# A hybrid SSD, pooling and expert layer on one core: expert outputs added into the residual by accumulating DMAs, weights of ranked experts loaded after the first gathers

## The chip, the cores and the metric

The kernel runs on one core of a Trainium2 chip. The metric is the device time of one execution in microseconds (us). The engines are TensorE (PE; its weight loads are shown as PEld), VectorE (DVE), ScalarE (ACT), GpSimd (POOL) and SyncE (SP). DMAs are issued by SP, ACT and POOL, each on a queue of its own, and run on 16 DMA engines. An indirect DMA takes a table of row numbers from on-chip memory, and POOL issues it.

## What is computed

One layer over 640 tokens of 1024 features (128 context, 512 latent), all float32. A first half (modulated norm, projections, two-way SSD scan, pooling mixer, output projection) leaves a residual `x`. The second half, which the change is about, routes each token to two of 16 experts and adds their weighted sum, gated, to the residual; a last norm gives the output:

```python
combine = jnp.sum(one_hot(idx, N_EXPERTS) * gate[..., None], axis=1)   # two gates a token
g = jnp.einsum("td,edf->tef", t, w_gate)
u = jnp.einsum("td,edf->tef", t, w_up)
a = silu(g) * u * combine[..., None]
out = jnp.einsum("tef,efd->td", a, w_down)
x = x + gate2 * out          # gate2: one row for context tokens, one for latent tokens
y = rmsnorm(x, final_norm_w)
```

## The kernel before

**Slots and tiles.** After routing, DVE ranks the experts by their number of tokens and gives every (token, choice) pair a slot. A tile holds up to 128 slots of one expert; a unit is 32 slots. The experts run in a fixed order of ranks (`RUN_ORDER`), 51 units in all: 47 written out (`UNITS`, 16 tiles in `TILES`), and a tile of 4 units in a loop that repeats if experts have more tokens than their space (here it runs once). `token_of` holds, for each tile, the token number of each slot.

**One tile.** POOL gathers the tile's token rows from `h2_dram` with an indirect DMA (`gather`, L1376) into one of two buffers `xg`; it issues the gather of tile q as soon as tile q-2 has been turned (`s_xtp`, L1383). PE turns the rows feature-major (`turn_tokens`, L872) during the last unit of the tile before; ACT and DVE copy the result out of PSUM (L1175, L1837).

**One unit.** PE multiplies by gate and up weights (`gate_up`, L882: two stretches with the turn of the unit before between them), ACT applies silu (L1182), DVE multiplies (`activate`, L1841), PE turns the activation (L887), ACT copies it (L1179), PE multiplies by the down weights (`down`, L895) into one of two PSUM banks, and DVE copies the 128x256 result (32 slots by 4 column groups of 256 on 128 partitions) into a buffer `yo` of its tile (`copy_out`, L1844). PE's `down` of unit v waits until the output of unit v-2 has been copied (`s_yo`). DVE works strictly in this order: `activate(v)`, then `unit_out(v-1)`.

**Storing.** When a tile's last unit is copied, ACT stores the tile with four DMAs, one per column group, to `slot_out` in DRAM (`store`, L1187; the loop's tile L1236). There are two `yo` buffers: the first copy into one waits until the tile two before has been stored:

```python
def unit_out(v):
    n, q, u = UNITS[v]
    dve.wait_ge(s_dn, v + 1)
    if u == 0 and q >= 2:
        dve.wait_ge(s_yst[q % 2], 64 * (q // 2))      # L1850
    copy_out(v, q % 2, u)
```

**Weights.** Each expert has six chunks of 1 MB (`w_exp`); 16 chunk slots stand on chip. Expert 0's are loaded ahead. As soon as the order of experts is known (`s_own`, L488), SP loads the next ones (L495), ten chunks at once and then each when its slot has been used for the last time.

**The end.** When all tiles are stored, POOL gathers for each of the five token tiles the two rows of each token from `slot_out` (10 indirect DMAs, L1401). ACT weights the first rows (`weigh`, L1243), DVE mixes (`mix`, L1892), POOL multiplies by gate2 (L1409), DVE adds to the residual `x1` on chip (`residual`, L1901), ACT sums squares and takes the root (L1251, L997), DVE normalises into one of two buffers `fout` (`final_norm`, L1909), and SP stores `y_out` (L504).

**Earlier places that the change touches.** POOL clears the rows of `slot_out` that no slot fills with 24 DMAs (L1344, at 170 to 182 us). After each output-projection tile ACT stores h2 (`copy_h2`, L1148). At the end of routing DVE builds one-hot tables (L1811 to L1813), PE sums them into token numbers (L861, 20 matmuls), and DVE casts these to `token_of` (L1829), which releases POOL's first gathers.

Of the kernel before, what the change touches and what calls it, by code (L numbers as in the profile page):

```python
# [23 lines left out]
F32 = mybir.dt.float32  # L24
# [41 lines left out]
SLOTS = MAX_TILES * P  # L66
# [20 lines left out]
UNFILLED = [(t * P + size * TU, (t + 1) * P) for t, size in TILES if size < 4]  # L87
UNFILLED += [(t * P, (t + 1) * P) for t in range(MAIN_TILES, MAX_TILES)]
# [13 lines left out]
C_STACK, C_KEY, C_TAB = 722, 754, 770  # L102
C_ALL = 818
# [24 lines left out]
def trunk_kernel(nc, consts, bconsts, vecs, rows, inv, fnorm, x, states0, w_ring, w_late, b_late, w_dt,  # L128
                 w_pool, w_router, w_exp, y_out, s_out):
    ctx = ExitStack()  # L130
    with ctx:
# [9 lines left out]
        slot_out = nc.dram_tensor("slot_out", [SLOTS, D], F32).ap()  # L141
# [213 lines left out]
        s_yst = [sem(f"expert_outputs_stored_{i}") for i in range(2)]  # L355
        s_yg = [sem(f"expert_rows_gathered_{j}") for j in range(NJ)]
        s_ya = sem("first_rows_weighted")
        s_mix = sem("expert_rows_mixed")
        s_gm = sem("mixed_rows_gated")
        s_fin = sem("final_sum_ready")  # L360
# [25 lines left out]
        yo = [t.rearrange("p (u c) -> p u c", u=4) for t in (zf[:, 4 * D:5 * D], bf_[:, 0:D])]  # L386
# [3 lines left out]
        g2row = rf[:, 0:2 * D].rearrange("p (c d) -> p c d", c=2)  # L390
        fnrow = rf[:, 2 * D:3 * D]
        fout = [rf[:, 3 * D + i * D:3 * D + (i + 1) * D] for i in range(2)]
        ygb = ex[:, 0:2 * NJ * D].rearrange("p (n d) -> p n d", d=D)
        ri = sb("ri", [P, 64], I32)
        idx = sb("idx", [P, 2], I32)
# [7 lines left out]
        in_tile = zf[:, 3328:3328 + 2 * NJ * MAX_TILES].rearrange("p (i n) -> p i n", n=MAX_TILES)  # L403
# [7 lines left out]
        def _(sp):  # L411
# [76 lines left out]
            sp.wait_ge(s_own, 1)  # L488
            for n in range(1, E - 1):
# [7 lines left out]
            with sp.Fori(0, k_loop) as i:  # L497
                e = sp.value_load(ri[0:1, bass.ds(i + E, 1)], min_val=0, max_val=E - 1)
                sp.wait_ge(s_lrel, i + 1)
                for c in range(6):  # L500
                    sp.dma_start(slots_[LOOP_SLOT + c], w_exp[e, c]).then_inc(s_ch[LOOP_SLOT + c], 16)
            for j in range(NJ):
                sp.wait_ge(s_fo, j + 1)
                sp.dma_start(y_out[j * P:(j + 1) * P, :], fout[j % 2]).then_inc(s_ost[j % 2], 16)  # L504
# [6 lines left out]
        def _(pe):  # L511
# [348 lines left out]
            for i in range(2 * NJ):  # L860
                mm = pe.matmul(psb[5][:, 0:MAX_TILES], at_pos[:, i, :], in_tile[:, i, :],  # L861
# [57 lines left out]

            pe.wait_ge(s_xg[0], 16)  # L920
# [72 lines left out]
        def _(act):  # L993
# [148 lines left out]
            def copy_h2(j):  # L1142
# [5 lines left out]
                act.dma_start(h2_dram[j * P:(j + 1) * P, :], h2bufs[j % 2]).then_inc(s_h2s[j % 2], 16)  # L1148

# [16 lines left out]
            copy_h2(NJ - 1)  # L1166
            exp_logits(1)
            warm(ACT.Silu)

# [13 lines left out]

            def store(rows, b, size):

                for g in range(AG):
                    act.dma_start(slot_out[rows, g * 256:(g + 1) * 256].rearrange("(u t) c -> t u c", t=TU),  # L1187
                                  yo[b][g * TU:(g + 1) * TU, 0:size, :]).then_inc(s_yst[b], 16)
# [3 lines left out]
            for v, (n, q, u) in enumerate(UNITS):  # L1192
# [12 lines left out]
                if v >= 2 and UNITS[v - 2][2] == TILES[UNITS[v - 2][1]][1] - 1:  # L1205
                    qs = UNITS[v - 2][1]
                    t, size = TILES[qs]
                    act.wait_ge(s_yo, v - 1)
                    store(slice(t * P, t * P + size * TU), qs % 2, size)
# [3 lines left out]
            act.wait_ge(s_yo, NV)  # L1213
            t, size = TILES[NQT - 1]
            store(slice(t * P, t * P + size * TU), (NQT - 1) % 2, size)
            act.dma_start(fnrow, fnorm.to_broadcast([P, D])).then_inc(s_fn, 16)
# [28 lines left out]
            for j in range(NJ - 1):  # L1245
                weigh(j)
# [775 lines left out]
```

## Time and profile before

| what | value |
|---|---|
| time, median of 3 runs | 986.18 us (985.52 to 986.61) |
| profiled execution, its own time | 986.62 us |
| its span, first to last instruction | 984.4 us |
| busy: PE, DVE, ACT, POOL | 858.6, 368.0, 166.6, 221.8 us |
| DMA traffic over the span | 199.61 MB, mean 203 GB/s |
| experts, first PE turn of tokens to last copy out | 626.85 to 937.06 us |
| after the experts, to the end of the span | 47.3 us |

The stretch before 600 us is the first half and the routing begins at its end; the experts take some 310 us; the tail gathers, mixes, norms and stores. A row of the timeline gives start, length, engine, line, what it writes and reads, and in brackets the idle time of the engine before it with what ended that.

### The profile page before, as it was taken

What the parts mean: (1) busy time and instruction counts of PE and PEld (TensorE: products, weight loads), DVE (VectorE), ACT (ScalarE), POOL (GpSimd) and SP (SyncE); (2) the same over time, 40 slices, a digit from 0 to 9 for tenths busy, and PEclk for the clock granted to TensorE, in tenths of its full rate; (3) what the DMA queues carried; (4) which work ended last, traced back from release to release, by engine and by line L of the source; (5) the groups of instructions that cost most, each with busy time, mean ns of one, the idle gap of its engine ahead of it and who ended that gap; (6) DMA issues with size and microseconds to landing.
All of it is one profiled execution on the core that took longest, in us unless ns stands there. A gap on an engine that the chain in (4) does not pass through costs nothing.

```text
span 984.4 us, 18375 instructions
## 1 busy us (share of the span) xinstructions
PE 858.6 (87%) x7969; PEld 491.2 (50%) x7969; DVE 368.0 (37%) x651; ACT 166.6 (17%) x367; POOL 221.8 (23%) x255
## 2 busy tenths in 40 slices
PE   1899999999899999999999972499998999999900
PEld 1655555555545555554445542255555555555500
DVE  1431004543683799873223527011111111111128
ACT  4121001121312222220000210011111111111123
POOL 0169999400233333320000000100000000000062
PEclk9999999999999999999999985699999999999965
DMA  9932755950310000295000011989989999998262
GB/s 357 414 137 95 311 194 188 351 216 7 123 42 0 1 1 1 94 371 200 21 22 21 21 62 46 380 334 357 362 308 418 336 390 399 388 406 311 82 234 107
DMA packets 39551, 199.61 MB, mean 203 GB/s; under 512 B 4720, under 2 KB 13872, under 8 KB 22320
## 3 DMA queue, kind: packets, MB, share of 16 engines
q1 hardware_dynamic: 22032, 162.82, 42.1%
q0 software_dynamic: 6224, 22.55, 6.5%
q10 hardware_dynamic: 11216, 13.08, 4.0%
q8 instruction: 63, 1.03, 0.4%
q14 instruction: 16, 0.13, 0.0%
HBM read 176.37 MB, written 22.05 MB: 202 GB/s over the span
## 4 chain that ended last, share of the span: by engine, by line
PE 55%; DVE 11%; DMA 3%; issue 2%; POOL 1%; ACT 1%; ACTq 0%; POOLq 0%; DVEq 0%
PE bank L882 18%; PE bank L782 13%; PE bank L895 8%; PE bank L646 6%; DMA slot_out<-yT 2%; PE bank L872 2%; PE bank L887 1%; DVE ex L1559 1%; PE bank L684 1%; DVE xs L1612 1%; DVE ex L1892 1%; DMA yT<-h_dram,token_of 1%; PE bank L835 1%; POOL ex L1367 1%; DVE ex L1575 1%
## 5 line engine op out<-in xcount | busy, mean ns | idle before, releaser
L574 PE MATMUL bank<-hT,ring 128*128 128x512 f32 (+1 forms) x640 | 180.7, 442 | 1.5 <-DMA ring<-w_ring 1.5
L574 PEld LDWEIGHTS bank<-hT,ring 128*128 128x128 f32 x640 | 96.6, 194 | 73.5 <-issue 71.0
L1376 POOL DMA_INDIRECT yT<-h_dram,token_of x17 | 16.6, 979 | 423.6 <-PE bank L872 236.4
L1841 DVE TENSOR_TENSOR bcT<-bcT,bank 128x128 f32<-128x128 f32 x51 | 14.6, 287 | 176.3 <-ACT bcT L1182 176.3
L646 PE MATMUL bank<-ring,hT 128*128 128x512 f32 x160 | 75.2, 604 | 4.5 <-DVE ex L1583 2.2
L882 PE MATMUL bank<-ex,yT 128*32 128x256 f32 x1216 | 74.7, 388 | 0.8 <-DVE yT L1837 0.8
L882 PE MATMUL bank<-ring,yT 128*32 128x256 f32 x1248 | 75.1, 381 | 0.0
L782 PE MATMUL bank<-ring,yT 128*128 128x512 f32 x160 | 70.2, 593 | 0.8 <-DVE yT L1621 0.8
L1367 POOL TENSOR_TENSOR ex<-ex,dts 128x512 f32<-128x512 f32 x40 | 44.3, 1108 | 99.9 <-ACT ex L1116 99.7
L882 PEld LDWEIGHTS bank<-ex,yT 128*32 128x32 f32 x1216 | 37.5, 112 | 27.3 <-issue 2.4
L882 PEld LDWEIGHTS bank<-ring,yT 128*32 128x32 f32 x1248 | 37.9, 110 | 25.4 <-issue 0.3
L782 PEld LDWEIGHTS bank<-ring,yT 128*128 128x128 f32 x160 | 30.3, 190 | 38.8 <-issue 37.8
L646 PEld LDWEIGHTS bank<-ring,hT 128*128 128x128 f32 x160 | 28.2, 190 | 31.6 <-issue 25.9
L1575 DVE TENSOR_TENSOR ex<-ex,gT 128x512 f32<-128x512 f32 x40 | 31.9, 797 | 24.3 <-POOL ex L1367 24.3
L895 PE MATMUL bank<-ex,bcT 128*32 128x256 f32 x640 | 38.2, 379 | 0.0
L1116 ACT ACTIVATE ex<-bank 128x512 f32<-128x512 f32 x40 | 23.9, 597 | 83.5 <-PE bank L733 83.4
L1179 ACT ACTIVATE bcT<-bank 128x128 f32<-128x128 f32 x51 | 14.2, 277 | 139.0 <-PE bank L887 139.0
L1746 DVE COPY bcT<-bank 128x512 f32<-128x512 f32 x10 | 6.9, 692 | 78.2 <-PE bank L782 78.2
L782 PE MATMUL bank<-ring,uT 128*128 128x512 f32 x80 | 36.1, 597 | 0.0
L782 PE MATMUL bank<-hT,uT 128*128 128x512 f32 x80 | 35.3, 594 | 0.8 <-DVE bcT L1600 0.8
L1351 POOL TENSOR_TENSOR ex<-xs,dts 128x1024 f32<-128x1024 f32 x8 | 15.1, 1901 | 87.4 <-DVE xs L1500 70.0
L1512 DVE SCALAR_TENSOR_TENSOR ex<-ex,vec 128x643 f32<-128x643 f32 x36 | 33.0, 916 | 1.3
(286 smaller groups left out, 1185.2 us busy)
## 6 DMA issues: line engine op xcount, KB each, us to landing
ex<-w_exp SPq DMA_DIRECT2D x36, 1024.0 KB, 11.8
ring<-w_exp SPq DMA_DIRECT2D x36, 1024.0 KB, 12.6
ring<-w_ring SPq DMA_DIRECT2D x13, 2048.0 KB, 10.5
yT<-w_late SPq DMA_DIRECT2D x16, 1024.0 KB, 6.5
hT<-w_exp SPq DMA_DIRECT2D x12, 1024.0 KB, 13.7
uT<-w_exp SPq DMA_DIRECT2D x12, 1024.0 KB, 15.6
slot_out<-ex POOLq DMA_DIRECT2D x13, 512.0 KB, 16.6
ex<-x SPq DMA_DIRECT2D x5, 512.0 KB, 8.0
```

Of the source, the lines that this page charges most:

```text
L574: mm = pe.matmul(o, w[:, k, (f % 4) * P:(f % 4 + 1) * P], hT[:, k, lo:hi], start=(k == 0), stop=(k == KT - 1))
L646: mm = pe.matmul(psb[6][:, :], hT[:, k, j * P:(j + 1) * P], w[:, k, :], start=(k == 0), stop=(k == KT - 1), skip_group_check=True)
L782: mm = pe.matmul(out_bank(j, hf_, c)[:, :], (yT, uT)[c][:, k, j * P:(j + 1) * P], w[:, k, :], start=(k == 0), stop=(k == KT - 1), skip_gro ...
L872: mm = pe.transpose(psb[2 + k // 4][:, (k % 4) * P:(k % 4) * P + rows], xg[b][0:rows, k * P:(k + 1) * P], ident[0:rows, 0:rows])
L882: mm = pe.matmul(psb[v % 2][g * TU:(g + 1) * TU, 0:256], xgT[b][:, k, u * TU:(u + 1) * TU], w[:, kk, g, :], start=(k == 0), stop=(k == KT ...
L895: mm = pe.matmul(psb[6 + v % 2][g * TU:(g + 1) * TU, 0:256], aT[v % 2][:, fb * TU:(fb + 1) * TU], w[:, kk, g * 256:(g + 1) * 256], start=( ...
L1116: act.activation(wbuf(i)[:, :, :, :], psb[4 + i % 2][:, :].rearrange("p (h d t) -> p h d t", h=2, d=2), ACT.Exp).then_inc(s_ex, 1)
L1351: return pool.tensor_tensor(out.rearrange("p (h d) -> p h d", d=HD), x_.rearrange("p (h d) -> p h d", d=HD), factors.unsqueeze(2).to_broad ...
L1367: pool.tensor_tensor(wbuf(i)[:, :, :, :], wbuf(i)[:, :, :, :], dt_h.unsqueeze(3).to_broadcast([P, 2, 2, P]), ALU.mult).then_inc(s_wd, 1)
L1376: pool.indirect_dma_start(xg[b][0:size * TU, :], None, h2_dram, bass.IndirectOffsetOnAxis(ap=numbers, axis=0), bounds_check=TOK - 1, oob_i ...
L1512: ins = stt(cacc[f % 2], xpad[f % 2][:, q:q + 643], wq, cacc[f % 2], ALU.mult, ALU.add)
L1575: step(tt(w.rearrange("p h d t -> p (h d) t"), w.rearrange("p h d t -> p (h d) t"), gT[:, j, hh // HG, :].unsqueeze(1).to_broadcast([P, 4, ...
```

## The change

**Adding in DRAM.** The residual `x1` is also stored to a DRAM tensor `x2_dram` (by ACT in `copy_h2`, five DMAs of 512 KB; the tensor has 128 spare rows for slots that hold no token). Seen as rows of 256 columns, 4 to a token, it takes each unit's 128x256 output by one indirect DMA from POOL that adds (`add_rows`). Before an output leaves PSUM, DVE multiplies it by gate and gate2: `weigh` makes a 128x256 row of weights by two instructions, and `copy_out` is now a multiplication (three DVE instructions of 128x256 instead of one). Outputs go to `YB = 4` buffers of one unit each.

**What waits for what.** POOL issues the add of unit v when its output stands (`s_yo`) and the add of unit v-1 has landed (`s_sc`). DVE's copy of unit v waits until the add of unit v-4 has landed. The gather of tile q+2 now stands in POOL's program behind the add of the unit before tile q's first. The stores to `slot_out`, its gathers, `weigh`, `mix`, `residual` and the 24 clearing DMAs are gone (one clearing DMA is left). At the end SP waits for the last add, loads the five tiles from `x2_dram`, and norm and store follow.

**Routing.** The table that PE sums gets twice the columns (token code and gate: 60 instead of 30), DVE does two more instructions before it and two more behind it, ahead of the first gather. Beside the first gathers, PE spreads the values over partitions (16 matmuls) and DVE makes weights and row numbers of all units.

**Weights.** SP loads the ranked experts' chunks only when both first gathers have landed (`s_xg`).

```diff
@@ SP
             sp.wait_ge(s_own, 1)
+            sp.wait_ge(s_xg[0], 16)
+            sp.wait_ge(s_xg[1], 16)
             for n in range(1, E - 1):
...
+            sp.wait_ge(s_sc, k_loop * 64 + 16 * NV)
+            for j in range(NJ):
+                sp.dma_start(x1[:, j, :], x2_dram[j * P:(j + 1) * P, :]).then_inc(s_x2[j], 16)
@@ ACT
                 act.dma_start(h2_dram[j * P:(j + 1) * P, :], h2bufs[j % 2]).then_inc(s_h2s[j % 2], 16)
+                act.dma_start(x2_dram[j * P:(j + 1) * P, :], x1[:, j, :]).then_inc(s_acc, 16)
...
-                    act.wait_ge(s_yo, v - 1)
-                    store(slice(t * P, t * P + size * TU), qs % 2, size)
...
-            for j in range(NJ - 1):
-                weigh(j)
             for j in range(NJ):
-                act.wait_ge(s_fin, j + 1)
+                act.wait_ge(s_x2[j], 16)
                 act.activation(junk_z, x1[:, j, :], ACT.Square, accum_out=stat[:, j:j + 1]).then_inc(s_fss, 1)
@@ POOL
-            for lo, hi in UNFILLED:
-                pool.dma_start(slot_out[lo:hi, :], zero_f[0:hi - lo, :]).then_inc(s_zero, 16)
+            pool.dma_start(x2_dram[TOK:TOK + P, :], zero_f).then_inc(s_zero, 16)
...
-            for q, (t, size) in enumerate(TILES):
-                if q >= 2:
-                    pool.wait_ge(s_xtp, q - 1)
+            x2_parts = x2_dram.rearrange("r (g n) -> (r g) n", g=AG)
+            def add_rows(numbers, b):
+                pool.indirect_dma_start(x2_parts, bass.IndirectOffsetOnAxis(ap=numbers, axis=0), yo[b], None,
+                                        bounds_check=(TOK + P) * AG - 1, oob_is_err=True,
+                                        compute_op=ALU.add).then_inc(s_sc, 16)
+            def gather_tile(q):
+                t, size = TILES[q]
                 gather(token_of[0:size * TU, t:t + 1], q % 2, size)
+            gather_tile(0)
+            gather_tile(1)
+            pool.wait_ge(s_acc, 16 * NJ)
+            pool.wait_ge(s_zero, 16)
+            pool.wait_ge(s_slot, 1)
+            for v, (n, q, u) in enumerate(UNITS):
+                if u == 0 and q + 2 <= NQT:
+                    pool.wait_ge(s_xtp, q + 1)
+                    gather_tile(q + 2)
+                pool.wait_ge(s_yo, v + 1)
+                if v >= 1:
+                    pool.wait_ge(s_sc, 16 * v)
+                c = TILES[q][0] * 4 + u
+                add_rows(rows_of[:, c:c + 1], v % YB)
             with pool.Fori(0, k_loop) as i:
                 pool.wait_ge(s_xg[LB], i * 16 + 16 * (NQT // 2 + 1))
+                pool.wait_ge(s_sc, i * 64 + 16 * NV)
...
@@ DVE
+            def weigh(done, ctx_col, lat_col):
+                ts(weight_q, g2q[:, 0, :], ctx_col, None, ALU.mult).then_inc(s_wq, 1)
+                dve.wait_ge(s_wq, done + 1)
+                stt(weight_q, g2q[:, 1, :], lat_col, weight_q, ALU.mult, ALU.add).then_inc(s_wq, 1)
+                dve.wait_ge(s_wq, done + 2)
-            def copy_out(v, b, u):
-                dve.tensor_copy(yo[b][:, u, :], psb[6 + v % 2][:, 0:256]).then_inc(s_yo, 1)
+            def copy_out(v):
+                tt(yo[v % YB], psb[6 + v % 2][:, 0:256], weight_q, ALU.mult).then_inc(s_yo, 1)
             def unit_out(v):
...
+                weigh(2 * v, w_ctx[:, c:c + 1], w_lat[:, c:c + 1])
                 dve.wait_ge(s_dn, v + 1)
-                if u == 0 and q >= 2:
-                    dve.wait_ge(s_yst[q % 2], 64 * (q // 2))
+                if v >= YB:
+                    dve.wait_ge(s_sc, 16 * (v - YB + 1))
```

In the loop tile the same waits stand with the loop's count added; there DVE, after the first `activate`, also waits until POOL has copied that tile's weights, which POOL does only when all 47 adds before have landed.

**How the order moves.** POOL's program before, from the first gather on (h_dram is h2_dram, token_of the table of row numbers, yT holds the buffers `xg`):

```order
L1376 DMA yT<-h_dram,token_of 128x1024
L1376 DMA yT<-h_dram,token_of 96x1024
L1376 DMA yT<-h_dram,token_of 128x1024
L1376 DMA yT<-h_dram,token_of 64x1024
L1376 DMA yT<-h_dram,token_of 128x1024
L1376 DMA yT<-h_dram,token_of 32x1024
```

The same stretch of POOL's program now (x_dram is x2_dram, its rows are 256 wide; yT,bcT hold the outputs and the row numbers):

```order
L1367 DMA yT<-h_dram,token_of 128x1024
L1367 DMA yT<-h_dram,token_of 96x1024
L1367 DMA yT<-h_dram,token_of 128x1024
L1376 DMA x_dram<-yT,bcT 3072x256 x4
L1367 DMA yT<-h_dram,token_of 64x1024
L1376 DMA x_dram<-yT,bcT 3072x256 x3
L1367 DMA yT<-h_dram,token_of 128x1024
L1376 DMA x_dram<-yT,bcT 3072x256 x4
```

Where POOL's queue held only gathers, one add per unit now stands between them, and each gather from the third on stands behind the adds of the tile before.

DVE's program at the beginning of the experts before (the first tile's tokens, then two activations ahead of the first copy out; bcT holds the activations, yT tokens and outputs):

```order
L1837 COPY yT<-bank 128x512
L1841 TENSOR_TENSOR bcT<-bcT,bank 128x128 x2
L1844 COPY yT<-bank 128x256
L1841 TENSOR_TENSOR bcT<-bcT,bank 128x128
L1844 COPY yT<-bank 128x256
L1837 COPY yT<-bank 128x4x96
```

And now:

```order
L1851 COPY yT<-bank 128x512
L1855 TENSOR_TENSOR bcT<-bcT,bank 128x128 x2
L1859 TENSOR_SCALAR bcT<-bcT 128x256
L1861 SCALAR_TENSOR_TENSOR bcT<-bcT 128x256
L1865 TENSOR_TENSOR yT<-bank,bcT 128x256
L1855 TENSOR_TENSOR bcT<-bcT,bank 128x128
```

Two instructions of 128x256 have come between the activation and the copy out, which has become a multiplication; the rest of a unit stands where it stood.

## Rows read from the trace of the kernel before

**Rows 1.** Windows: busy us (instructions) of each engine, granted clock, DMA share, GB/s.
```profile
640.00:740.00 100.00, 100.00 (x1697) 56.92 (x1693) 14.96 (x40) 12.17 (x40) 5.80 (x6) 1.00 0.89 341
740.00:760.00 20.00, 17.09 (x291) 9.70 (x283) 2.40 (x7) 1.99 (x6) 1.00 (x1) 1.00 1.02 419
760.00:900.00 140.00, 140.00 (x2376) 79.62 (x2368) 21.14 (x56) 17.14 (x56) 6.94 (x8) 1.00 0.97 377
```

**Rows 2.** Timeline of one unit: PE's down products, DVE's activation and copy out.
```profile
668.81 1.91 PE L895 MATMUL bank<-ring,bcT 128*32 128x256 f32 x32
...
669.37 0.29 DVE L1841 TENSOR_TENSOR bcT<-bcT,bank 128x128 f32<-128x128 f32 x1 [3.64 <-ACT bcT L1182]
...
670.79 0.42 DVE L1844 COPY bcT<-bank 128x256 f32<-128x256 f32 x1 [1.13 <-PE bank L895]
...
674.39 1.91 PE L895 MATMUL bank<-ring,bcT 128*32 128x256 f32 x32
```

**Rows 3.** Timeline at the beginning of the experts.
```profile
610.22 0.46 DVE L1813 TENSOR_TENSOR yT<-yT,cst 128x300 f32<-128x300 f32 x1
...
610.79 4.47 PE L861 MATMUL bank<-yT 128*128 128x30 f32 x20 [11.99 <-DVEq L1814]
...
614.55 3.35 SPq L495 DMA_DIRECT2D ring<-w_exp  x6
...
617.20 1.10 POOL L1376 DMA_INDIRECT yT<-h_dram,token_of  x1 [186.94 <-issue]
...
626.85 1.97 PE L872 MATMUL bank<-cst,yT 128*128 128x128 f32 x8 [11.58 <-DMA yT<-h_dram,token_of]
629.59 1.02 POOL L1376 DMA_INDIRECT yT<-h_dram,token_of  x1 [10.01 <-PE bank L872]
...
640.79 0.42 DVE L1844 COPY yT<-bank 128x256 f32<-128x256 f32 x1 [1.13 <-PE bank L895]
```

**Rows 4.** Line L1376 (token gathers, 630 to 904 us): issue time on POOL; time to landing.
```profile
L1376 POOL DMA_INDIRECT yT<-h_dram,token_of x15: 923/959/1017, 629.6 to 869.5; - x15
...
DMA to landing us min/median/max: 5.0/9.3/10.4
```

**Rows 5.** Tile slot_out, 640 to 880 us: the stores beside the weight loads.
```profile
DMA to landing us min/median/max: 5.5/10.2/16.4
```

**Rows 6.** Line L1401 (gathers from slot_out, no weight loads beside them).
```profile
DMA to landing us min/median/max: 4.3/6.0/6.1
```

**Rows 7.** Tile slot_out, 905 to 925 us: four stores after the last weight load.
```profile
DMA to landing us min/median/max: 1.9/2.0/2.1
```

**Rows 8.** DMA queues, 640 to 900 us: packets, MB, share of the window; SP's queue.
```profile
q1 hardware_dynamic: 11541, 84.06, 81.1%
```

**Rows 9.** Timeline where a copy out waits for a store.
```profile
757.39 0.42 DVE L1844 COPY yT<-bank 128x256 f32<-128x256 f32 x1 [10.60 <-DMA slot_out<-yT]
...
758.06 0.33 PE L887 MATMUL bank<-cst,bcT 128*128 128x128 f32 x1 [2.91 <-DVE bcT L1841]
```

**Rows 10.** Timeline at the first use of a ranked expert's weights.
```profile
652.64 1.05 PE L882 MATMUL bank<-ring,yT 128*32 128x256 f32 x16
```

**Rows 11.** Timeline of the tail: last copy out, last tile's sum, root, norm.
```profile
936.64 0.42 DVE L1844 COPY yT<-bank 128x256 f32<-128x256 f32 x1 [2.13 <-PE bank L895]
...
978.38 1.06 ACT L1251 ACTIVATE yT<-xs 128x1024 f32<-128x1024 f32 x1 [2.31 <-DVE xs L1901]
...
979.35 0.19 ACT L1251 ACTIVATION_READ_ACCUMULATOR yT<-xs 128x1 f32 x1
...
979.57 0.29 ACT L997 ACTIVATE stat<-stat,eps_col 128x1 f32<-128x1 f32 x1
979.89 0.16 DVE L1906 RECIPROCAL stat<-stat 128x1 f32<-128x1 f32 x1
980.09 1.28 DVE L1909 SCALAR_TENSOR_TENSOR ring<-xs,stat,ring 128x1024 f32<-128x1024 f32 x1
```

**Rows 12.** Line L504 (stores of the output, 512 KB each).
```profile
DMA to landing us min/median/max: 2.6/2.6/2.6
```

More of the change, by code:

```diff
@@ L354, in trunk_kernel @@
         s_yo = sem("expert_outputs_copied")
[L355 to L360, printed above, removed]
+        s_acc = sem("residual_stored")
+        s_g2 = sem("gate2_rows_loaded")
+        s_rep = sem("slot_values_spread")
+        s_slot = sem("slot_weights_ready")
+        s_here = sem("loop_slot_values_ready")
+        s_sc = sem("expert_outputs_added")
+        s_wq = sem("output_weights_ready")
+        s_x2 = [sem(f"final_sum_{j}_loaded") for j in range(NJ)]
         s_fss = sem("final_squares_summed")
@@ L385, in trunk_kernel @@
         xgT = [zf[:, (2 + i) * D:(3 + i) * D].rearrange("p (k t) -> p k t", k=KT) for i in range(2)]
-        yo = [t.rearrange("p (u c) -> p u c", u=4) for t in (zf[:, 4 * D:5 * D], bf_[:, 0:D])]
+        yo = [zf[:, 4 * D + i * 256:4 * D + (i + 1) * 256] for i in range(YB)]
+        g2q = bf_[:, 0:512].rearrange("p (c n) -> p c n", c=2)
+        per_slot = bf_[:, 512:512 + 2 * MAX_TILES]
+        weight_q = bf_[:, 640:896]
         sg = [bf_[:, D + i * P:D + (i + 1) * P] for i in range(2)]
@@ L389, in trunk_kernel @@
         aT = [bf_[:, D + 512 + i * P:D + 512 + (i + 1) * P] for i in range(2)]
[L390 to L393, printed above, removed]
+        rows_of = bf_[:, 1792:1792 + 4 * MAX_TILES].bitcast(I32)
+        w_ctx = bf_[:, 1912:1912 + 4 * MAX_TILES]
+        w_lat = bf_[:, 2032:2032 + 4 * MAX_TILES]
+        slot_tmp = bf_[:, 2152:2152 + 8 * MAX_TILES].rearrange("p (u n t) -> p u n t", u=4, n=2)
+        here = bf_[:, 2400:2408].rearrange("p (n u) -> p n u", n=2)
+        fnrow = gtf[:, 0:D]
         ri = sb("ri", [P, 64], I32)
-        idx = sb("idx", [P, 2], I32)
+        idx = sb("idx", [P, 5], I32)
         token_of = sb("token_of", [P, MAX_TILES + 1], I32)
@@ L918, in unit_down @@
                 mm.then_inc(s_dn, 1)
+            for u in range(4):
+                for g in range(AG):
+                    mm = pe.matmul(psb[5][g * TU:(g + 1) * TU, 256 + u * 64:256 + u * 64 + 2 * MAX_TILES],
+                                   ident[:, u * TU:(u + 1) * TU], per_slot, start=True, stop=True)
+            mm.then_inc(s_rep, 1)
             pe.wait_ge(s_xg[0], 16)
@@ L1166, in _ @@
             copy_h2(NJ - 1)
+            for g in range(AG):
+                act.dma_start(g2q[g * TU:(g + 1) * TU, :, :], ada_rows[3:4, :, g * 256:(g + 1) * 256].to_broadcast(
+                    [TU, 2, 256])).then_inc(s_g2, 16)
             exp_logits(1)
             warm(ACT.Silu)
+            act.wait_ge(s_lg, NJ)
+            act.dma_start(fnrow, fnorm.to_broadcast([P, D])).then_inc(s_fn, 16)
             act.wait_ge(s_rt, 1)
@@ L1182, in silu_gate @@
                 act.activation(sg[v % 2], psb[v % 2][:, 0:P], ACT.Silu).then_inc(s_sg, 1)
[L1184 to L1188, printed above, removed]
             act.wait_ge(s_xtp, 1)
@@ L1212, in _ @@
             copy_act(NV - 1)
[L1213 to L1216, printed above, removed]
-            act.dma_start(g2row, ada_rows[3:4].to_broadcast([P, 2, D])).then_inc(s_row2, 16)
             LB = NQT % 2
```

137 lines of the change are left out of this document (61 added, 76 removed).

## Prediction

> **What bounds the kernel now.** I read the windows first. While the experts run, PE is busy without a gap from 640 to 900 us but for 2.9 us near 750, and the DMA engines are at 0.89 to 1.02 of their time all along [rows 1]. So in this stretch PE is the bound, and the DMA engines have nearly nothing to spare. One unit shows in the timeline: from one group of down products to the next PE takes 5.58 us (668.81 to 674.39), and DVE waits 1.13 us between an activation and the copy out behind it [rows 2]. 51 units of 5.58 us are 285 us.
>
> Two stretches are not PE's. At the beginning PE waits 11.6 us for the first token gather, which POOL issues at 617.20 and which lands 9.6 us later, because SP has issued ten weight chunks just ahead of it, the first at 614.55 [rows 3]. And after the last copy out (936.64) nothing is left for PE; the tail lasts until 984.4 [rows 11].
>
> The third thing to see is what a small DMA takes. POOL's token gathers land 9.3 us (median; 5.0 to 10.4) after their issue while the weights stream [rows 4], ACT's stores 10.2 us (5.5 to 16.4) [rows 5]. Without weight loads beside them, the first gather of 512 KB in the tail lands after 4.3 us [rows 6], a store after 1.9 to 2.1 us [rows 7]. The kernel before mostly doesn't mind, since it waits for a store two tiles later; once it does, and then DVE's copy out stands 10.6 us and PE 2.9 us behind it [rows 9]. The change puts such a landing into every unit.
>
> **The change part by part.**
>
> *Tail.* The gathers, `weigh`, `mix` and `residual` go. What follows the last add: SP issues five loads of 512 KB, the first landing after some 2.6 us (a store of this size; a load isn't shown alone) [rows 12]; ACT takes 1.06 + 0.19 + 0.29 = 1.54 us for each tile, 7.7 for five, more than the 1.25 us in which 512 KB pass at 419 GB/s [rows 1, 11], so ACT sets the pace; then 0.16 + 1.28 us of DVE and 2.6 us of the store [rows 11, 12]. With 0.3 us for SP to wake and 0.7 for handovers and the end: 15.3 us from the landing of the last add to the end of the span.
>
> *Beginning.* DVE's two new instructions ahead of the table cost 0.17 and 0.46 us (as L1813 [rows 3]), those behind it two times 0.2, and I add 0.2 for PE's wider table: the first gather goes out 1.2 us later, at 618.4. No weight chunk is then in the queues, so it lands after 4.3 us instead of 9.6: PE turns tokens at 622.8 instead of 626.85, a gain of 4.0 us. Beside the gather, PE's 16 spreading matmuls (two passes each, 0.22 us a pass as in L861 if none overlap: 7 us) and six short DVE instructions must be done; four column groups can run at once, so I cost them at nothing; without that cover PE would be up to 4 us later.
>
> *Weights 9 us later.* They start at about 624 instead of 614.55. Their first use is at 652.64 [rows 10], and now at 648.6; the first six chunks need 16 us (2.64 each, below). Hidden, and nothing else is queued on SP.
>
> *Earlier parts.* Five more stores on ACT (0.35 us each, where ACT waits for DVE), 23 fewer on POOL at 170 us: PE waits for neither there. Nothing.
>
> *DVE in a unit.* Two more instructions of 128x256, at 0.42 us each as the copy of that size [rows 2]: 0.85 us with their handover, in a gap of 1.13 us. Nothing, and if the gap were gone, the second PSUM bank covers it.
>
> *The stall of 2.9 us at 758* [rows 9] goes with the stores.
>
> *The chain of adds.* This decides. POOL issues add v when add v-1 has landed; the copy out of unit v waits for add v-4; PE's `down` waits for copy v-2. So four buffers only delay the moment when PE feels the chain: in the long run a unit takes the longer of 5.58 us and one add from issue to issue. An add's period is POOL's wake (PE's turn ends at 628.82, POOL's instruction starts at 629.59: 0.77 us [rows 3]), its 0.96 us of issue [rows 4], and the way to the landing. No row shows an adding DMA, so I bound it.
>
> - Without loads: at least a 128 KB store, 1.9 us with 0.32 of issue changed for POOL's 0.96, so 2.5; at most the 512 KB gather's 4.3. It is nearest to the gather, which POOL also issues from a table; 384 KB less are 0.9 us less, reading the old row gives some back: 3.6. Period 3.3 to 5.1, taken 4.4.
> - Beside loads: at least the 5.0 of the quickest gather, at most its 10.4; the median 9.3, a little less for rows of a quarter of the size: 9.0. Period 5.8 to 11.2, taken 9.75.
>
> The weights stream on SP's queue for 81.1% of 260 us for 80 chunks (84.06 MB) [rows 8], 2.64 us a chunk, 237 us for all 90; 14.5 us of that lie ahead of the first add. So 223 us of the chain lie beside loads, whatever its length: 223 / 9.75 = 23 adds. The other 28 run at 4.4 us: 123 us. Together 346 us, more than PE's 285, so the chain is the bound and PE waits. To this come 4 us for the gathers that now stand in POOL's order between the adds, and 4 us at the loop tile, where DVE stands until all adds before have landed: 354 us.
>
> The Trainium skill, "DMA: Bandwidth & Descriptors", section on the anatomy of a DMA on the gpsimd path, fits such a DMA at about 2.0 us plus its bytes over 436e3, which for 128 KB is an estimate of 2.3 us. The gathers beside loads at 9.3 us speak against using it here. By it the chain would hide, which is the first rival.
>
> *Sum.* The first copy out came 14.4 us after the first turn (640.79 + 0.42 against 626.85 [rows 3]), so the first add starts at 622.8 + 14.4 + 0.8 = 638; the last lands at 638 + 354 = 992; the end is at 992 + 15.3 = 1007.3. The tail gives back 32 us of 47, the beginning 4, the stall 2.9; the chain takes some 62. The median of the runs is 1.8 us over the profiled span (986.18 against 984.4): 1009 us.
>
> **The rivals.**
>
> *The adds hide (faster).* If an add beside loads has a period under about 6 us, PE keeps its 5.58. Then the last copy out is at 622.8 + 310.2 - 2.9 = 930, the last add lands at 934.5, the end is at 950. One thing comes late next: the gather of the tile after rank 1's single-unit tile now stands behind an add and has one unit's time left, so PE waits some 4 us: 954, and 956 as a median. For it: one landing of 5.0 us [rows 4], and the sparse row of rows without loads. Against it: the median of 9.3, with DMA shares of 0.9 and more. The time is that of before where the chain is 331 us with all else, that is at a period beside loads of 7.9 us; below that it is faster. The estimate by the skill's fit falls into this case.
>
> *The add itself is dearer.* It reads the old row and writes the sum, which no row shows. With 2 us more on every add, periods of 11.75 and 6.4: 19 adds beside loads and 32 at 6.4, 428 + 8 us, the end at 1089 and 1091 as a median. For it: nothing but the unknown; against it: adds of 128 KB move a quarter of a gather.
>
> *The first gather isn't quicker.* If the new stores of the residual or the wider table hold it back, the 4 us at the beginning are lost, and PE's start is as before: 1013. Likewise late weights cannot cost more than the 9 us by which they start later.
>
> **How the numbers follow.** The chain binds as costed, period beside loads 7.9 to 11.2: 0.56; this case alone reaches from 986 to 1045. The adds hide wholly or mostly: 0.30, from 953 to 984. The dearer add: 0.10. A draw, where tail and chain cancel: 0.04. No change means within 0.2% (2 us), about what a measurement of this kernel can tell. So faster 0.31, same 0.04, slower 0.65. For 8 in 10 the range leaves out the quickest part of the first rival and the end of the second: 957 to 1064.
>
> **What would show it.** Right: DVE's copy out (the multiplication behind the weights) idle behind DMA x_dram in most units, PE's busy share between 640 and 940 near 0.8, the adds' landings in two groups near 4 and 9 us, POOL idle behind DMA x_dram, and the last add near 990. Wrong: PE still at 100% there with the last copy out near 930 (first rival), landings over 8 us also where no weights load (second), a first turn of tokens later than 624 (third), or PE waiting for the weight tiles.

## The result and the profile after

The changed kernel takes **1041.17 us** (median of 4 runs, 1039.94 to 1045.61) against 986.39 us for the kernel before (4 runs, 985.52 to 986.70). The ratio is 1.0565, with a 95% interval of 1.0532 to 1.0598: slower by 54.8 us. Forecast were 1009 us, slower by 22.8, in a range of 957 to 1064. The sign and the mechanism were forecast, the size was less than half of what came.

The profiled execution has a span of 1038.1 us. First the beginning of the experts, from the timeline; it answers to [rows 3]:

```profile
617.31 1.10 POOL L1367 DMA_INDIRECT yT<-h_dram,token_of  x1 [187.96 <-issue]
...
621.94 1.97 PE L882 MATMUL bank<-cst,yT 128*128 128x128 f32 x8 [4.39 <-DMA yT<-h_dram,token_of]
...
624.46 3.38 SPq L502 DMA_DIRECT2D ring<-w_exp  x6
```

The gather is issued at 617.31 and PE turns the tokens at 621.94 instead of 626.85, with the first weight chunk behind them. The end of the span, from the timeline; it answers to [rows 11]:

```profile
1018.42 1.55 POOL L1376 DMA_INDIRECT x_dram<-yT,idx  x1 [3.20 <-DMA x_dram<-yT,idx]
1022.18 2.50 SPq L511 DMA_DIRECT2D xs<-x_dram  x5
1026.04 1.06 ACT L1243 ACTIVATE yT<-xs 128x1024 f32<-128x1024 f32 x1 [10.60 <-DMA xs<-x_dram]
```

The last add lands at 1022.16, and 15.9 us later the span ends; before, 47.3 us followed the last copy out. Between these two places lies the loss. The windows of the same stretches as [rows 1] (columns as there):

```profile
640.00:760.00 120.00, 101.33 (x1636) 56.70 (x1626) 27.62 (x74) 11.88 (x39) 26.05 (x18) 0.91 0.85 311
760.00:900.00 140.00, 107.37 (x1681) 59.80 (x1685) 27.25 (x72) 12.37 (x40) 33.93 (x24) 0.85 0.85 295
```

PE was busy for 140.00 of 140 us from 760 to 900; now for 107.37. The DMA engines are less busy too, 0.85 against 0.97. Neither is the bound any more. What is shows in the page's line on the chain that ended last, and in its costliest groups (busy, mean ns, then idle time ahead with its main releaser):

```profile
DMA x_dram<-yT,bcT 25%; PE bank L792 13%; PE bank L656 6%; PE bank L892 4%; DMA yT<-h_dram,token_of 2%; PE bank L905 2%; DVE ex L1568 1%; PE bank L694 1%; DVE xs L1621 1%; PE bank L845 1%; POOL ex L1358 1%; PE bank L882 1%; DVE ex L1584 1%; PE bank L758 1%; DMA x_dram<-yT,idx 1%
...
L1376 POOL DMA_INDIRECT x_dram<-yT,bcT x47 | 73.7, 1568 | 278.7 <-DMA x_dram<-yT,bcT 165.5
...
L882 PE MATMUL bank<-cst,yT 128*128 128x128 f32 (+3 forms) x144 | 22.3, 313 | 67.8 <-DMA yT<-h_dram,token_of 67.8
...
L1865 DVE TENSOR_TENSOR yT<-bank,bcT 128x256 f32<-128x256 f32 x51 | 21.7, 425 | 67.0 <-DMA x_dram<-yT,bcT 50.1
```

A quarter of the span's last chain is the landing of adds (x_dram is the DRAM tensor of sums). POOL waits 165.5 us for them, DVE's copy out 50.1 us, and PE's turn of tokens 67.8 us for gathers, which raises a question that a run settles below. (Most of the rest of POOL's 278.7 us is put down to DVE's copy out, but at only 4 of the 50 adds behind the first did that output come after the landing ahead; mostly it had stood for 10 us and more.) What one add takes, from the answer on L1376, first from 637 to 700 us, beside weight loads, then from 975 to 1000 us, without:

```profile
L1376 POOL DMA_INDIRECT x_dram<-yT,bcT x7: 1544/1558/1609, 637.6 to 698.7; - x7
...
DMA to landing us min/median/max: 7.0/9.3/10.0
...
L1376 POOL DMA_INDIRECT x_dram<-yT,bcT x5: 1552/1552/1558, 976.3 to 995.3; - x5
...
DMA to landing us min/median/max: 3.8/3.8/4.4
```

The instruction itself takes POOL 1.56 us (a gather 1.0), landing 9.3 or 3.8 us after its start. Add by add, the next one starts 0.82 us after the landing in nearly all cases: the 51 adds are one chain without a gap, but for one of 7.1 us at 777 us and three at the loop's tile, 4.0 us together. From the first start (637.61) to the last landing (1022.16) it is 384.5 us.

### The profile page after: what moved, and what is told of

Same layout as the page of the kernel before. It is cut to its first block, busy times and chain, and to the rows that moved or that the text cites. A ratio compares the mean times of both kernels' runs of the same rounds, so it can differ in the third digit from the quotient of the medians.

```text
span 1038.1 us, 18638 instructions
## 1 busy us (share of the span) xinstructions
PE 876.3 (84%) x8001; PEld 498.3 (48%) x8001; DVE 391.5 (38%) x751; ACT 160.4 (15%) x362; POOL 269.7 (26%) x272
## 3 DMA queue, kind: packets, MB, share of 16 engines
q8 instruction: 63, 1.03, 0.4%
## 4 chain that ended last, share of the span: by engine, by line
PE 32%; DMA 28%; DVE 9%; issue 4%; POOL 2%; ACT 1%; POOLq 0%; DVEq 0%; ACTq 0%
DMA x_dram<-yT,bcT 25%; PE bank L792 13%; PE bank L656 6%; PE bank L892 4%; DMA yT<-h_dram,token_of 2%; PE bank L905 2%; DVE ex L1568 1%; PE bank L694 1%; DVE xs L1621 1%; PE bank L845 1%; POOL ex L1358 1%; PE bank L882 1%; DVE ex L1584 1%; PE bank L758 1%; DMA x_dram<-yT,idx 1%
## 5 line engine op out<-in xcount | busy, mean ns | idle before, releaser
L1376 POOL DMA_INDIRECT x_dram<-yT,bcT x47 | 73.7, 1568 | 278.7 <-DMA x_dram<-yT,bcT 165.5
L892 PE MATMUL bank<-ring,yT 128*32 128x256 f32 x1248 | 80.1, 400 | 0.0
L882 PE MATMUL bank<-cst,yT 128*128 128x128 f32 (+3 forms) x144 | 22.3, 313 | 67.8 <-DMA yT<-h_dram,token_of 67.8
L892 PE MATMUL bank<-ex,yT 128*32 128x256 f32 x1216 | 77.1, 398 | 0.9 <-DVE yT L1851 0.9
L882 PEld LDWEIGHTS bank<-cst,yT 128*128 128x128 f32 (+3 forms) x144 | 17.9, 176 | 75.7 <-DMA yT<-h_dram,token_of 72.8
L1865 DVE TENSOR_TENSOR yT<-bank,bcT 128x256 f32<-128x256 f32 x51 | 21.7, 425 | 67.0 <-DMA x_dram<-yT,bcT 50.1
## 6 DMA issues: line engine op xcount, KB each, us to landing
uT<-w_exp SPq DMA_DIRECT2D x12, 1024.0 KB, 13.5
```

What stands on the lines that cost most here:

```text
L882: mm = pe.transpose(psb[2 + k // 4][:, (k % 4) * P:(k % 4) * P + rows], xg[b][0:rows, k * P:(k + 1) * P], ident[0:rows, 0:rows])
L892: mm = pe.matmul(psb[v % 2][g * TU:(g + 1) * TU, 0:256], xgT[b][:, k, u * TU:(u + 1) * TU], w[:, kk, g, :], start=(k == 0), stop=(k == KT ...
L1376: pool.indirect_dma_start(x2_parts, bass.IndirectOffsetOnAxis(ap=numbers, axis=0), yo[b], None, bounds_check=(TOK + P) * AG - 1, oob_is_er ...
L1865: tt(yo[v % YB], psb[6 + v % 2][:, 0:256], weight_q, ALU.mult).then_inc(s_yo, 1)
```

## The experiments

Ratios are to runs of the kernel before on the same chip, with their 95% intervals. The theory going in: the chain of landings is the bound, and a landing is long because of the weight loads beside it. Its rivals: the addition itself is dear; the gathers, which now stand behind adds, are the cause; the DMA engines' bandwidth is.

### The gathers two units earlier

```diff
-                if u == 0 and q + 2 <= NQT:
-                    pool.wait_ge(s_xtp, q + 1)
-                    gather_tile(q + 2)
+                for k in (range(3) if v == 0 else (v + 2,)):
+                    if k < NV and UNITS[k][2] == 0 and UNITS[k][1] + 2 <= NQT:
+                        pool.wait_ge(s_xtp, UNITS[k][1] + 1)
+                        gather_tile(UNITS[k][1] + 2)
```

> The changed kernel with each token gather from the fifth or so on issued two units earlier in POOL's program (ahead of the add of the unit two before its tile's predecessor ends); the serial waits between adds stay. Theory (the chain of landings): TensorE's 63 us of waits for gathers are only where it stands while the chain sets the pace; they move to the copies out of PSUM, and only the one gap of the chain at 777 us (7.1 us) and little else goes: 1028 to 1041 us. Rival (gathers behind adds are the cause): the 63 us go, 975 to 1000 us.

Measured: 1039.07 us, ratio 1.0501 (1.0469 to 1.0533). From the view of waits, 622 to 1020 us (total us, times, longest), with the copy out at L1866:

```profile
DVE yT L1866 <- DMA x_dram<-yT,bcT: 186.9, 34, 8.8
...
PE bank L897 <- DVE bcT L1856: 29.1, 11, 13.5
PE bank L882 <- DMA yT<-h_dram,token_of: 25.8, 3, 17.5
```

In the changed kernel the same view has:

```profile
PE bank L882 <- DMA yT<-h_dram,token_of: 67.8, 10, 17.2
DVE yT L1865 <- DMA x_dram<-yT,bcT: 50.1, 13, 8.3
```

PE waits for gathers 25.8 us in 3 places instead of 67.8 in 10, and the time hardly moves: the copy out waits 186.9 us for adds where it waited 50.1, and PE waits for DVE. The chain is as long as in the changed kernel, 637.47 to 1021.32 us: the gap of 7.1 us is gone from it, but 30 adds took over 4.5 us to land and not 28. So most of the 67.8 us in the page's row on PE name the place where PE happened to stand, not a cause.

### Fewer weights beside the adds

```diff
+                    cols = 2048 if m < NSLOT else 256
-                    sp.dma_start(slots_[m % NSLOT], w_exp[e, c]).then_inc(s_ch[m % NSLOT], 16)
+                    sp.dma_start(slots_[m % NSLOT][:, 0:cols], w_exp[e, c, :, 0:cols]).then_inc(s_ch[m % NSLOT], 16)
```

The loop's six chunks are cut in the same way.

> The changed kernel with all expert chunks from the 17th on cut to an eighth of their columns (128 KB instead of 1 MB; the rest of a slot keeps older weights, so those experts' outputs are others). All adds, waits and TensorE's work stay. Theory (the chain of landings): nearly all adds land in 3.8 us, a period of 4.6 us is under TensorE's 5.58, so TensorE binds: last add near 935 us, 945 to 960 us. Rival (the addition is dear wherever it runs, loads or not): the chain stays over TensorE's pace, 1000 us or more.

Measured: 954.97 us, ratio 0.9687 (0.9655 to 0.9720). The answer on the adds (here L1377), with POOL's idle time by releaser:

```profile
L1377 POOL DMA_INDIRECT x_dram<-yT,bcT x47: 1542/1557/1604, 636.0 to 909.2; - x47
...
  DVE yT L1866: 138.9, 33
  DMA x_dram<-yT,bcT: 52.0, 13
...
DMA to landing us min/median/max: 3.7/3.9/9.5
```

Same adds, same serial waits; the median landing is 3.9 us, and in 33 waits of POOL it is the output that comes last (here rightly so: at 36 adds the copy out ended after the landing ahead). The chain alone is no bound, beside loads it is. With the run that waits between tiles only (below), this carries the main conclusion.

### The addition taken out

```diff
                 pool.indirect_dma_start(x2_parts, bass.IndirectOffsetOnAxis(ap=numbers, axis=0), yo[b], None,
-                                        bounds_check=(TOK + P) * AG - 1, oob_is_err=True,
-                                        compute_op=ALU.add).then_inc(s_sc, 16)
+                                        bounds_check=(TOK + P) * AG - 1, oob_is_err=True).then_inc(s_sc, 16)
```

> The changed kernel with the addition taken out of its 51 indirect DMAs: each writes its 128 rows of 1 KB over what stands there (so the output holds only the last write to a row). Theory (the chain of landings): a small DMA is slow beside the weight loads whatever it does, since its packets queue behind weight packets; the addition costs only the longer packets (101 ns against 46 ns of a plain 1 KB store, 8 an engine: about 0.45 us an add). 51 x 0.45 = 23 us less: 1005 to 1030 us, landings near 8.7 us beside loads and 3.3 without. Rival (the addition itself is dear): landings beside loads fall below 6 us and the kernel below 985 us. Rival (gathers behind adds): 1030 to 1041 us, no change.

Measured: 981.22 us, ratio 0.9926 (0.9902 to 0.9950). The time is where the rival (the addition is dear) put it, below 985 us, but the landings are where neither side did. The answer on L1376 from 637 to 680 us (beside loads) and from 723 to 733 us (two without, one beside):

```profile
L1376 POOL DMA_INDIRECT x_dram<-yT,bcT x6: 986/1023/1062, 637.1 to 675.8; - x6
...
DMA to landing us min/median/max: 6.6/6.8/7.3
...
L1376 POOL DMA_INDIRECT x_dram<-yT,bcT x3: 986/986/1097, 723.9 to 730.6; - x3
...
DMA to landing us min/median/max: 2.4/2.5/7.1
```

Landings fall from 9.3 to 6.8 us beside loads, where the theory had 8.7 and the rival less than 6, and from 3.8 to 2.5 without. So the addition is a part of the price: 1.3 us without loads, 2.5 beside them, 0.54 to 0.57 of each in POOL's issue. The loads are the larger part: without the addition a landing still takes 4.3 us longer beside them. It changes more than the arithmetic, as the page's row of POOL's queue shows (packets, MB, share), first of the changed kernel, then of this one:

```profile
q0 software_dynamic: 9680, 13.51, 6.8%
```

```profile
q0 software_dynamic: 4784, 13.51, 4.0%
```

The same bytes take 4896 fewer packets, 96 fewer for each of 51 adds: with the addition each row of 1 KB is a packet (128), without it four rows go as one of 4 KB (32).

### Half of the rows

```diff
-... numbers, axis=0), yo[b], None,
+... numbers, axis=0), yo[b][0:64, :], None,
-                add_rows(rows_of[:, c:c + 1], v % YB)
+                add_rows(rows_of[0:64, c:c + 1], v % YB)
```

The loop's adds are cut in the same way.

> The changed kernel with each add taking the first 64 of its 128 rows only (column groups 0 and 1 are added, the outputs of groups 2 and 3 are left out). Theory (an add's packets take turns with weight packets): beside loads the first packet still comes 4.75 us after issue, but four packets an engine follow instead of eight: landings near 7.2 us instead of 9.2, near 3.2 without loads. A period beside loads holds weight packets for 0.8 to 0.85 of it, so their 225 us make about 33 periods of 8.0 us (265 us), 17 of 4.0 (68), and 10 for the gathers and the loop: 343 us against 384 measured: 995 to 1012 us. Rival (an adding DMA has a price of its own, whatever its rows): landings stay near 9 and 3.8 us, 1030 us or more.

Measured: 1001.50 us, ratio 1.0118 (1.0052 to 1.0183), inside what the theory gave. The answer on L1376 from 639 to 725 us (beside loads), then from 725 to 741 us:

```profile
L1376 POOL DMA_INDIRECT x_dram<-yT,bcT x10: 1407/1421/1509, 640.0 to 716.4; - x10
...
DMA to landing us min/median/max: 6.9/7.8/8.7
...
L1376 POOL DMA_INDIRECT x_dram<-yT,bcT x4: 1402/1414/1421, 726.0 to 737.8; - x4
...
DMA to landing us min/median/max: 3.0/3.1/3.2
```

With the addition kept, half the rows save 0.7 us without loads and 1.5 beside them: a part of the price goes with the number of packets, and more so where weight packets stand against them. The total came as the theory had it, its split did not: 29 adds of 8.5 us beside loads instead of 33 of 8.0, 22 of 4.0 without instead of 17, and 14 us of gaps instead of 10.

### Weight packets of 4 KB

```diff
-                    sp.dma_start(slots_[m % NSLOT], w_exp[e, c]).then_inc(s_ch[m % NSLOT], 16)
+                    for h in range(2):
+                        sp.dma_start(slots_[m % NSLOT][:, h * 1024:(h + 1) * 1024], w_exp[e, c, :, h * 1024:(h + 1) * 1024]).then_inc(s_ch[m % NSLOT], 16)
```

Expert 0's and the loop's loads are cut in the same way, and PE waits for 32 a chunk.

> The changed kernel with every expert weight chunk loaded by two DMAs of half the columns, so in packets of 4 KB instead of 8 KB; same bytes, same adds. Theory (the chain of landings, by packets that take turns): beside loads an add's first packet comes 2.6 us later than without loads and its eight packets an engine are spread over 4 us instead of 1.3; with weight packets of half the length both excesses halve, landings beside loads fall from 9.2 to about 6.3 us, and 28 such adds give 28 x 2.9 = 80 us back, until TensorE binds in places: 955 to 990 us. Rival (shared bandwidth: an add waits for a share of bytes, or loads slow down): landings stay near 9 us, 1030 to 1050 us. Rival (the addition itself is dear): unchanged, 1030 to 1045 us.

Measured: 1024.98 us, ratio 1.0349 (1.0315 to 1.0383): 2.2 points less than the changed kernel's ratio, some 21 us (the two profiled executions differ by 13.5 us), about a quarter of what the theory gave. Landings beside loads, from the answer on the adds (here L1379), 637 to 724 us:

```profile
DMA to landing us min/median/max: 7.2/7.9/8.7
```

7.9 us and not 6.3. By the packets' own records, over the adds that took more than 4.5 us to land, the spread of an add's packets shrank as expected: in the median from 3.4 to 2.2 us, against 1.2 without loads. The first packet's delay did not: 4.8 us after the start in both kernels, against 2.1 without loads. It is the same 2.6 us with half of the rows (4.6 against 2.0) and without the addition (4.2 against 1.6). What makes these 2.6 us, no run here shows. A second step of the theory failed too: it held the number of such adds at 28, but 34 took over 4.5 us, since beside the same loads shorter periods are more periods.

The Trainium skill, "DMA: Bandwidth & Descriptors", section on queues, rings and completion order, has each DMA engine go round between its queues a packet at a time, and counts some 9 to 17 descriptors to a packet. That the spread shrinks with shorter weight packets and with fewer rows would agree if a packet of the profile (8 KB of weights, 1 KB of an add) were such a turn, which no run here shows; the constant delay doesn't follow from it.

As a control the same cut in the kernel before:

> The kernel before with every expert chunk loaded by two DMAs of half the columns (4 KB packets), as a control: does the packet length alone change anything? Theory: TensorE binds, the loads carry the same bytes; only the first gather (9.6 us) and the stall of 2.9 us behind a store gain a little: 981 to 988 us, no change that can be measured or a gain of a few us. Rival (4 KB packets slow the loads): TensorE waits for weights, 990 us or more.

Measured: 983.40 us, ratio 0.9967 (0.9939 to 0.9994), a gain of some 3 us: PE's stall of 2.9 us at 758 [rows 9] isn't there in its trace. So small packets slow nothing, and most of what they gave the changed kernel is due to the small DMAs that stand in its chain.

### The wait on the weights, alone and taken away

```diff
             sp.wait_ge(s_own, 1)
+            sp.wait_ge(s_xg[0], 16)
+            sp.wait_ge(s_xg[1], 16)
```

> The kernel before with only the wait of the changed kernel on the weights: SP loads the ranked experts' chunks when both first gathers have landed. Theory: the first gather, issued at 617.2 us, lands after 4.3 to 4.8 us instead of 9.6, TensorE starts 5 us sooner, and the weights, first used 26 us later, are in time: 978 to 984 us. Rival (weights late): TensorE waits for chunks that came 9 us later and the gain is lost or more: 985 to 995 us.

Measured: 983.87 us, ratio 0.9966 (0.9947 to 0.9985). In its timeline the gather is issued at 621.88 (routing ended 4.7 us later in this execution) and PE follows 5.3 us behind, where it was 9.65 us [rows 3]:

```profile
621.88 1.10 POOL L1378 DMA_INDIRECT yT<-h_dram,token_of  x1 [186.94 <-issue]
...
627.14 1.97 PE L874 MATMUL bank<-cst,yT 128*128 128x128 f32 x8 [7.18 <-DMA yT<-h_dram,token_of]
```

The other way, the changed kernel without these two lines:

> The changed kernel without the wait on the weights. Theory (the chain of landings): TensorE starts 5 us later, but the chunks are then 9 to 10 us further ahead, so about one add fewer meets loads (10.0 - 4.7 = 5.4 us less): the two cancel, 1036 to 1047 us. Rival (the wait makes weights late): faster by 9 us or more, under 1033 us.

Measured: 1045.04 us, ratio 1.0586 (1.0558 to 1.0614). The time lies where both sides of the theory's sum put it, but not for its reason: the first add starts at 643.88 and the last lands at 1028.17, 384.3 us as with the wait. Earlier weights took no add out of the loads: 30 took over 4.5 us to land, two more than with the wait. The wait is worth some 3 us in the kernel before; in the changed one the ratios say 2, with intervals that overlap.

### Waits between tiles only

The 32 slots of a unit and the 128 of a tile belong to one expert, so no two units of a tile add to the same row. One semaphore a buffer keeps each wait exact:

```diff
-                if v >= 1:
-                    pool.wait_ge(s_sc, 16 * v)
+                if v >= 1 and u == 0:
+                    for b in range(YB):
+                        if adds(v, b):
+                            pool.wait_ge(s_sc[b], adds(v, b))
...
-                    dve.wait_ge(s_sc, 16 * (v - YB + 1))
+                    dve.wait_ge(s_sc[v % YB], 16 * (v // YB))
```

Here `adds(v, b)` is 16 times the number of units before v that use buffer b; the loop's waits change in the same way.

> The changed kernel with the wait between adds kept only where it is needed, between tiles: the units of one tile hold one expert's slots, so their rows differ, and POOL issues their adds as the outputs stand; the first add of a tile waits for all before. One semaphore a buffer. Theory (the chain of landings): a tile of four units then needs one landing and not four, about 12 us for two units and 18 us for four beside loads against 11.2 and 22.3 us of TensorE, so TensorE binds nearly everywhere: the last add lands near 945 us, the tail of 16 us stays, 950 to 975 us, which is less than the kernel before. Rival (the addition itself is dear, its engines being busy with it): 51 adds need as long as before, 1020 to 1041 us. Rival (gathers behind adds): TensorE's waits for gathers of some 60 us stay, 1010 to 1041 us.

Measured: **963.61 us**, ratio 0.9734 (0.9704 to 0.9764). The landings are as long as ever, by the answer on the adds (here L1379) from 622 to 960 us:

```profile
DMA to landing us min/median/max: 3.7/9.4/11.2
```

But POOL waits for one only ahead of a tile's first add, 16 times instead of 50. From 640 us on PE has one wait left in the unrolled tiles:

```profile
745.45 1.97 PE L885 MATMUL bank<-cst,yT 128*128 128x128 f32 x8 [9.36 <-DMA yT<-h_dram,token_of]
```

It stands behind the one-unit tile, where the prediction's first rival had 4 us for the adds that hide; here it is 9.36. To remove it, the gathers one add earlier:

> The version that waits between tiles only (963.6 us), with each later token gather issued one add earlier in POOL's program: ahead of the last add of the tile before, which for a one-unit tile waits for a landing. Theory: TensorE's one wait there, 9.4 us for a gather at 745 us, goes, and nothing comes in its place: 952 to 957 us. Rival (the wait moves on: the adds themselves then hold TensorE up at that place): 959 to 964 us.

Measured: 965.55 us, ratio 0.9775 (0.9748 to 0.9801): a miss, nothing is gained, and the time is above what the rival gave too. PE's waits from 640 us to the loop's tile:

```profile
742.91 1.23 PE L885 MATMUL bank<-cst,yT 128*128 128x128 f32 x8 [4.08 <-DMA yT<-h_dram,token_of]
888.04 0.88 PE L885 MATMUL bank<-cst,yT 96*128 96x96 f32 x8 [1.92 <-DMA yT<-h_dram,token_of]
902.59 0.33 PE L900 MATMUL bank<-cst,bcT 128*128 128x128 f32 x1 [0.66 <-DVE bcT L1866]
908.71 1.09 PE L885 MATMUL bank<-cst,yT 128*128 128x128 f32 x8 [2.20 <-DMA yT<-h_dram,token_of]
```

8.9 us in four places instead of 9.4 in one. Both versions with weight packets of 4 KB:

> The version that waits between tiles only, with 4 KB weight packets. Theory (turns): gathers and adds land 1 to 1.5 us sooner beside loads, so of TensorE's one wait there (9.4 us, for a gather behind an add that itself waited for a landing) 3 to 5 us go: 957 to 962 us against 963.6. Rival (nothing is left for small packets to give, or they slow the loads): 962 to 970 us.

Measured: 961.05 us, ratio 0.9734 (0.9682 to 0.9786). The time lies in the theory's range, but the ratio is that of 8 KB packets (0.9734): no gain is shown, though PE's one wait shrank from 9.36 to 6.55 us in the profiled execution.

> The same with the gathers one add earlier. Theory: the 8.2 us that TensorE still waited there in three or four places for gathers and adds fall to 3 us or less: 954 to 961 us. Rival: 962 us or more, as with 8 KB packets.

Measured: **955.51 us**, ratio 0.9675 (0.9624 to 0.9726). In the unrolled tiles the timeline has no wait of PE any more from 640 us on, and the windows show it full:

```profile
640.00:760.00 120.00, 119.92 (x2025) 68.18 (x2021) 33.29 (x87) 14.71 (x48) 38.76 (x27) 1.00 1.05 380
760.00:900.00 140.00, 140.00 (x2367) 79.75 (x2362) 40.00 (x105) 17.43 (x56) 44.63 (x31) 1.00 1.05 374
```

So the change's idea, with waits between tiles only, gathers one add earlier and weight packets of 4 KB, is 3.3% faster than the kernel before, and 2.8% faster than that kernel with the same packets (983.40). The DMA engines then move 380 and 374 GB/s where they moved 311 and 295 in the changed kernel, so their bandwidth, the last of the rivals, was not its bound.

## Why the prediction came out as it did

Against the span before, the parts are: PE's first turn 4.9 us earlier; from there to the last landing 400.2 us (621.94 to 1022.16) where it was 310.2 to the last copy out; the tail 15.9 us where it was 47.3. That is -4.9 + 90.0 - 31.4 = 53.7 us, the difference of the spans.

- **Beginning: right.** Forecast 622.8, measured 621.94. The gather went out at 617.31 where 618.4 was forecast, but routing's end moves by more than that between executions (4.7 us in the run of the wait alone). What holds is the way from issue to turn, 4.63 us instead of 9.65. PE's spreading matmuls, costed at nothing, took 1.03 us beside it.
- **Weights later, DVE's two instructions, earlier parts at nothing: right** as far as the time shows; the wait on the weights costs neither kernel time.
- **Tail: right,** with two terms that offset each other. Forecast 15.3 us from the last landing, measured 15.9: ACT starts 3.9 us after the landing instead of 2.9, and takes 1.40 us a tile instead of 1.54.
- **The chain as the bound: right.** Fewer loads bring 955 us, waits between tiles only 964, with everything else kept. One sign of it came otherwise than written: DVE's copy out is idle behind adds 13 times and not in most units, since PE meets the chain first at the gathers behind the adds (10 times). With these gathers earlier it is 34 times, at the same time of the kernel.
- **The periods: nearly right, by bounds from gathers.** Forecast 9.75 us beside loads and 4.4 without; over the 51 adds, landing and 0.82 us of handover make 9.53 in the mean of 28 that took over 4.5 us to land, and 4.67 in the other 23.
- **The number of adds beside loads: wrong. This is the step that failed:** "223 / 9.75 = 23 adds", where 28 were slow. It takes for granted that weight packets fill the whole of such an add's period. The weights' amount was forecast well: from 637.6 to 1022.2 us their queue has 59.1% of the engines' time, 227 us:

```profile
q1 hardware_dynamic: 12373, 90.05, 59.1%
```

But these 227 us were spread over 28 adds of 9.53 us, 267 us, a share of 0.85 (by the packets' records 219 of the 227 lie in these periods). A part of the rest is the add's own packets, 8 a DMA engine at 0.10 us; that the remainder is gathers and the end of a burst of chunks, when the next slot isn't free, follows from the order of the kernel and is not measured apart. An add that meets only a part of a burst pays most of the price too: 5 of the 28 landed after 5.0 to 7.3 us.

So the forecast's 224 + 123 + 8 = 355 us became 267 + 107 + 11 = 385, the last landing needing no handover: 43 us more beside loads, 16 less without, 3 more in gaps. These 30 us are nearly the whole miss of 32; with the step as measured the sum is 1039. The mended step is no constant, though. The run with half of the rows had been forecast with a share of 0.8 to 0.85, 343 us, and has 347.9 (639.97 to 987.83). But counted as above its share is 0.92, so that its total agrees in part by luck; the share is 0.84 with 4 KB packets, 0.81 with the gathers earlier, 0.93 without the addition. All are below the 1 of the prediction; what sets them within 0.8 to 0.93 no run takes apart.

**The rivals.** The second ("the add itself is dearer") got a chance of 0.10 and is partly true. Against a plain write an adding DMA lands 1.3 to 2.5 us later, and without the addition the kernel would have been a little faster than before, at 981 us. The bounds had this in them unseen: that the period came out at 9.53 is in part luck, since gathers of up to 512 KB and 128 packets happen to land as late (9.3 us) as adds of 128 KB. The first rival was wrong on whether the adds hide. Its price for hidden adds, 956 us, is near the 955 of the run with fewer loads, where landings take 3.9 us as its condition wants; that the fastest version above comes to 955.5 is no test of it, since there landings are long and waits are fewer.

The estimate by the fit of the Trainium skill, "DMA: Bandwidth & Descriptors", section on the anatomy of a DMA on the gpsimd path, was 2.3 us. The trace agrees for the plain write without loads (2.5); the fit misses the add (3.8), and everything beside loads (6.8 and 9.3).

## What to carry to other kernels

A wait for a small DMA's landing, put into every step, must be priced by landings beside the traffic that will be there, and here the steps that paid it were more than traffic time divided by period, since the traffic filled only 0.8 to 0.93 of the periods. Ask first which of the waits the data needs: here only a change of tile needed one, and dropping the other two thirds turned a loss of 5.7% into a gain of 2.7%. A row that shows an engine waiting long for something (PE's gathers) names where the engine stood, and moving that something is a quick test whether it is the cause.

## What was not expected of the hardware

- An adding indirect DMA of 128 rows of 1 KB goes as 128 packets, the plain one as 32 of 4 KB; POOL needs 1.56 us to issue it against 0.99.
- Beside weight loads the first packet of an add came 4.8 us (median) after its start against 2.1 without, whether the weights went in packets of 8 KB or 4 KB; the 2.6 us between are the same with half of the rows and without the addition.
- The granted clock fell where PE waited: its mean from 760 to 900 us is 0.85 in the changed kernel, a mix of the levels of 1.2 and 2.4 GHz, where it was 1.00 before. Behind the longest wait there, 17.17 us, it was 0.50 (1.2 GHz) and the eight matmuls of a turn took 1.97 us; at the loop's end, at 1.00 (2.4 GHz), such a turn took 1.09 us. With the chain as the bound, the clock could cost little here; no run took it apart. The two turns from the timeline, then the windows around them:

```profile
775.47 1.97 PE L882 MATMUL bank<-cst,yT 128*128 128x128 f32 x8 [17.17 <-DMA yT<-h_dram,token_of]
...
1012.03 1.09 PE L882 MATMUL bank<-cst,yT 128*128 128x128 f32 x8
```

```profile
775.00:777.50 2.50, 2.03 (x12) 1.70 (x16) 0.02 (x1) 0.02 (x1) 1.37 (x2) 0.50 0.53 64
1011.00:1014.00 3.00, 2.25 (x36) 1.38 (x25) 2.05 (x6) 0.82 (x3) 0.33 (x1) 1.00 0.10 13
```
